# Windowed attention with four score buffers and a different order of work, and eleven small loads moved one stage earlier

## The reference

```
def neighbourhood_attention(u, rel_bias, na_idx, na_rel):
    ...
        sc = (jnp.einsum('bqhd,bqnhd->bhqn', qb, kb, preferred_element_type=jnp.float32) * scale
              + jnp.take(bias_flat, rel, axis=1))
        p = jax.nn.softmax(sc, axis=-1).astype(v.dtype)
        o = jnp.einsum('bhqn,bqnhd->bqhd', p, vb)
...
        oa = rms_norm(gqa_axial(...), g_out_a[l])
        ob = rms_norm(mla(...), g_out_b[l])
        oc = diff_attention(..., g_out_c[l], slopes, lambda_init)
        od = rms_norm(neighbourhood_attention(ud, d_rel_bias[l], na_idx, na_rel), g_out_d[l])
        mix = jnp.concatenate([oa, ob, oc, od], axis=-1) @ w_out[l]
        x = x + rms_norm(mix, norm_mix_post[l])
        h = rms_norm(x, norm_mlp_pre[l])
```

## Time and profile before

| what | value |
|---|---|
| median of 3 runs | 3023.75 us (3023.37 to 3025.94) |
| profiled execution | 3023.84 us, span 3022.0 us |
| PE, share of the span | 91% |
| DVE, ACT | 64%, 46% |
| stage D, layer 1 | 675.56 to 732.38 us |
| stage D, layer 2 | 2163.59 to 2220.43 us |
| idle time of PE before the output stage's first transposes | 12.3 us, 13.5 us |

### The profile page before, as it was taken

One profiled execution on the slowest core, in us unless ns is written; L12 is line 12 of the kernel. 1 busy time (PEld: TensorE's weight loads), 2 busy tenths in 40 slices (PEclk: granted clock), 3 DMA queues, 4 the chain that ended last, 5 costly groups with the idle time before them and its releaser, 6 DMA issues. The chain is left out here.

```text
span 3022.0 us, 37758 instructions
## 1 busy us (share of the span) xinstructions
PE 2740.4 (91%) x13872; PEld 2286.0 (76%) x13872; DVE 1931.9 (64%) x2856; ACT 1385.5 (46%) x2330; POOL 553.4 (18%) x487
## 2 busy tenths in 40 slices
PE   5998899887979999999879979988869799999997
PEld 4986888566758887888769859876658588878886
DVE  5612867886678887445774148669766888864457
ACT  4312766776343322443433147668654433334344
POOL 2122514780000000000021225248500000000000
PEclk7999999898989999999989989989989899999998
DMA  7232655543224444855533326754412244467555
GB/s 210 60 136 84 207 147 177 83 99 112 63 63 153 154 154 157 274 195 194 182 83 100 120 86 202 191 153 64 136 50 77 87 150 152 152 215 234 195 186 169
DMA packets 326941, 431.08 MB, mean 143 GB/s; under 512 B 82006, under 2 KB 207706, under 8 KB 326492
## 3 DMA queue, kind: packets, MB, share of 16 engines
q1 hardware_dynamic: 326736, 428.56, 46.1%
q10 hardware_dynamic: 12, 0.02, 0.0%
HBM read 288.00 MB, written 140.86 MB: 142 GB/s over the span
## 5 line engine op out<-in xcount | busy, mean ns | idle before, releaser
L1997 PE MATMUL f_ps<-dn_g 128*128 128x512 f32 x2688 | 617.1, 391 | 10.0 <-DVE dn_g L2228 10.0
L1997 PEld LDWEIGHTS f_ps<-dn_g 128*128 128x128 f32 x2688 | 505.4, 189 | 117.8 <-DVE dn_g L2228 7.2
L2228 DVE TENSOR_TENSOR dn_g<-dn_raw,dn_g 128x2048 fp32r<-128x2048 f32 x112 | 256.4, 2291 | 265.2 <-ACT dn_g L2077 265.2
L1987 PE MATMUL f_ps<-hc_h,up_w_h 128*128 128x512 f32 x896 | 352.5, 393 | 25.9 <-DVE up_w_l L2194 20.5
L2077 ACT ACTIVATE dn_g<-dn_raw 128x2048 fp32r<-128x2048 f32 x112 | 214.3, 1915 | 331.8 <-PE f_ps L1997 215.9
L1987 PE MATMUL f_ps<-hc_h,up_w_l 128*128 128x512 f32 x896 | 351.7, 393 | 0.0
L1987 PEld LDWEIGHTS f_ps<-hc_h,up_w_h 128*128 128x128 f32 x896 | 170.3, 190 | 63.1 <-DVE up_w_l L2194 27.5
L1987 PE MATMUL f_ps<-hc_ld,up_w_h 128*128 128x512 f32 x512 | 200.4, 391 | 0.0
L1987 PEld LDWEIGHTS f_ps<-hc_h,up_w_l 128*128 128x128 f32 x896 | 170.1, 190 | 35.8
L490 POOL TENSOR_TENSOR w_row_l<-w_row_first,w_row_h 128x512 fp32r<-128x512 f32 x12 | 14.9, 1281 | 904.4 <-ACT w_row_h L599 904.4
L1275 DVE CUSTOM_DVE_ANT_0 s_ps_c<-s_ps_c,distance 128x1024 f32<-128x1024 f32 x128 | 156.7, 1225 | 12.3 <-PE s_ps_c L1158 12.3
(11 more groups left out here) (297 smaller groups left out, 6461.7 us busy)
## 6 DMA issues: line engine op xcount, KB each, us to landing
act_blocks<-u_stage SPq DMA_DIRECT2D x32, 1792.0 KB, 6.6
dn_raw<-act_blocks SPq DMA_DIRECT2D x112, 512.0 KB, 3.9
mix<-in_w_down SPq DMA_DIRECT2D x128, 256.0 KB, 3.5
down_sums<-mix SPq DMA_DIRECT2D x128, 256.0 KB, 2.8
up_raw<-in_w_up SPq DMA_DIRECT2D x32, 1024.0 KB, 5.3
dn_raw<-down_sums SPq DMA_DIRECT2D x64, 512.0 KB, 4.8
dn_raw<-in_w_down SPq DMA_DIRECT2D x48, 512.0 KB, 4.6
w_raw<-in_w_in SPq DMA_DIRECT2D x16, 512.0 KB, 4.1
```

The source lines that it names most:

```text
L1987: last = nc.tensor.matmul(dst, wt[:, x % RING, k, :], tok, start=(opens[j] and k == 0 and i == 0), stop=(k == KT // 2 - 1 and i == 2), ski ...
L1997: last = nc.tensor.matmul(f_ps[:, bank0[pi] + i, :], lhs[:, n % 4, 0, q, i * P:(i + 1) * P], rhs[:, n % 4, 1, q, :], start=(down_opens[pi] ...
L2228: nc.vector.tensor_tensor(g_l[:, n % 4], dn_raw[:, n % 3], g_h[:, n % 4], ALU.subtract) \
```

## The change

D gets a stage function of its own, `window_stage`. The score tile is four buffers of one PSUM bank (before: two of two banks, of which 384 columns were used), `prob` has four buffers, and the waits follow from these. TensorE issues four `scores` first and then in each iteration turn(n), scores(n + 4), a half of `values`, `finish`; ScalarE runs two exponentials ahead and VectorE three maxima ahead. The eleven small loads are issued and waited for at the end of D's `fetch_out`; `g_col` and `out_li` have 1 KB of memory of their own for that. In the output stage VectorE multiplies `g_col` as its first instruction, with no wait.

```
+        def window_stage(mem, maps, tiles, mix_cols, mix, fetch, values_landed):
...
+            DEEP = 4
...
+                prob = mem.take("prob_d", [P, DEEP, 3 * P])
...
+                s_ps = ps(c, "s_ps_d", [P, DEEP, HALF])
+                t_ps = ps(c, "t_ps_d", [P, 2, HALF])
...
+                    def scores(n):
+                        m, i = n // NT, n % NT
+                        first, cnt = tiles[i][0:2]
+                        if n >= DEEP:
+                            pe.wait_ge(S["exp_done"], n - DEEP + 1)
...
+                    def turn(n):
+                        pe.wait_ge(S["exp_done"], n + 1)
+                        if n >= 2:
+                            pe.wait_ge(S["pt_lo"], n - 1)
...
+                    for n in range(DEEP):
+                        scores(n)
+                    for n in range(n_all + 4):
+                        if n < n_all:
+                            turn(n)
+                        if n + DEEP < n_all:
+                            scores(n + DEEP)
+                        if 0 <= n // 2 - 1 < n_groups:
+                            values(n // 2 - 1, n % 2)
+                        if n >= 4 and n % 2 == 0:
+                            finish(n // 2 - 2)
...
+                        act.wait_ge(S["max_done"], n + 1)
+                        if n >= DEEP:
+                            act.wait_ge(S["ptr_done"], n - DEEP + 1)
...
+                    exponential(0)
+                    exponential(1)
+                    for n in range(n_all + 2):
+                        if n + 2 < n_all:
+                            exponential(n + 2)
+                        if n < n_all:
+                            high(n)
+                        if n >= 3 and n % 2 == 1:
+                            lift(n // 2 - 1)
...
+                    for n in range(3):
+                        maximum(n)
+                    for n in range(n_all + 4):
+                        if n + 3 < n_all:
+                            maximum(n + 3)
+                        if n < n_all:
+                            low(n)
+                        if n >= NT + 3 and (n - 3) % NT == 0:
+                            divide((n - 3) // NT - 1)
...
+            oc = arena((136, 137))
+            g_col = oc.take("o_g_col", [P, KT])
+            out_li = oc.take("o_li", [P, 2])
...
                 for k in range(KT):
                     sp.dma_start(wo_raw[:, k, :], a["w_out"][layer][k * P:(k + 1) * P, :]).then_inc(S["w_landed0"], 16)
+                col = lambda v: v.rearrange("a p -> p a")
+                for j, name in ((0, "g_out_a"), (1, "g_out_b"), (3, "g_out_d")):
+                    for r in range(2):
+                        sp.dma_start(g_col[:, 2 * j + r:2 * j + r + 1], col(vec(name, r * P, (r + 1) * P))) \
+                            .then_inc(S["const_landed"], 16)
+                for j in range(2):
+                    for r in range(2):
+                        sp.dma_start(g_col[r * HD:(r + 1) * HD, 4 + j:5 + j], col(vec("g_out_c"))).then_inc(S["const_landed"], 16)
+                sp.dma_start(out_li[:, :], row_vector(vec("lambda_init"))).then_inc(S["const_landed"], 16)
                 sp.wait_ge(S["w_landed0"], 16 * KT)
+                sp.wait_ge(S["const_landed"], 16 * 11)
...
-            attention_stage("d", arena((-38, -24), (80, 104)), maps, tiles,
-                            lambda m: slice((12 + m) * HD, (13 + m) * HD), mix, fetch_out, 16)
+            window_stage(arena((-38, -24), (80, 104)), maps, tiles,
+                         lambda m: slice((12 + m) * HD, (13 + m) * HD), mix, fetch_out, 16)
...
-                om = arena((0, 48), (80, 92), (136, TOP))
+                om = arena((0, 48), (80, 92), (137, TOP))
...
-                g_col = om.take("o_g_col", [P, KT])
-                li = om.take("o_li", [P, 2])
...
-                    for j, name in ((0, "g_out_a"), (1, "g_out_b"), (3, "g_out_d")):
...
-                    sp.dma_start(li[:, :], row_vector(vec("lambda_init"))).then_inc(S["const_landed"], 16)
...
+                    nc.vector.tensor_scalar(g_col[:, 4:6], g_col[:, 4:6], out_li[:, 1:2], None, ALU.mult) \
+                        .then_inc(S["gain_done"], 1)
                     mix_sums(0)
-                    dve.wait_ge(S["const_landed"], 16 * 11)
-                    nc.vector.tensor_scalar(g_col[:, 4:6], g_col[:, 4:6], li[:, 1:2], None, ALU.mult) \
-                        .then_inc(S["gain_done"], 1)
                     mix_norm(0)
```

More of the change, by code:

```diff
@@ L1561, in _ @@
                 def _(sp):
-                    col = lambda v: v.rearrange("a p -> p a")
-                    for j, name in ((0, "g_out_a"), (1, "g_out_b"), (3, "g_out_d")):
[L1564 to L1569, removed]
-                    sp.dma_start(li[:, :], row_vector(vec("lambda_init"))).then_inc(S["const_landed"], 16)
                     def residual(t):
```

111 lines of the change are left out of this document (added).

## The result

The changed kernel takes 3003.11 us (median of 4 runs, 3001.53 to 3006.92), the kernel before beside it on the same chip 3023.56 us (4 runs, 3022.53 to 3025.94). The ratio is 0.9933, 95% interval 0.9916 to 0.9950: 20.45 us less, where 18.6 was forecast. The profiled execution took 3003.13 us with a span of 3001.5 us.

What follows compares the result with a forecast made beforehand. No engine is full: TensorE waits on a chain in D, and the output stage's reciprocal waits behind `o_li`. Savings of 12.0 (loads) and 6.6 (D), together 18.6, from 3023.8 give 3005 us, range 2998 to 3012.

Steps and rivals of the forecast that it cites:

- The likeliest case: Whole kernel: output stage and D both gain, 18.6 us together, giving 3005 us; chance 0.62.
- What bounds the kernel: In D, TensorE waits on a chain through ScalarE and VectorE; in the output stage, the first reciprocal stalls behind `o_li`.
- Loads moved, 12.0: Output stage: the first reciprocal waits only for the roots, saving 5.4 and 6.6 us in the two layers.
- D, 6.6: Stage D: the new order shortens waits before values, saving 3.3 us per layer, 1.06 per map.
- The chain of 1.44 us: In D, from an odd turn's end through ScalarE's copy and VectorE's subtraction to the values; claimed to stay the same.
- The buffers: Four one-bank score buffers and four `prob` in D: cost nothing; their possible effect on the clock was a rival.
- The chances: Whole kernel: forecast 0.62, rivals 0.16, 0.10, 0.08, 0.04; faster by over 0.2%: 0.95, cut to 0.93.
- the first three rivals: Only the output stage gains, 0.16; all of D's waits go, 0.10; the output stage gives part back, 0.08.
- Only the output stage gains: In D, ScalarE's exponentials delay the odd copies, so only the 12.0 us come: 3012 us; chance 0.16.
- All of D's waits go: In D, TensorE becomes the bound at 10.2 us per map, 14.2 saved there: 2997.6 us; chance 0.10.
- Part given back through the clock: Output stage: the 1.2 GHz stretch lasts longer as work comes earlier, 6 us back: 3011 us; chance 0.08.
- Slower, the clock falls in D: In D, many short gaps draw the clock down; with 60 us of low clock, 3035 us; chance 0.04.
- rival 4: The slower case: D's short gaps lower the clock, 3035 us with 60 us of it; chance 0.04.

Runs made afterwards that it cites:

- e1: The changed kernel with D's old stage function, so only the small loads and the g_col multiplication moved: 3011.33 us, ratio 0.9956.
- e2: The kernel before with only the new stage D, the small loads still in the output stage: 3016.80 us, ratio 0.9978.
- e5: The changed kernel with three score and prob buffers instead of four, maxima still three ahead: 3007.84 us, ratio 0.9954.
- e10: The changed kernel with two buffers, exponentials one ahead, and the maximum two tiles ahead in front of low on VectorE: 3008.23 us, ratio 0.9955.
- e3: The changed kernel with its four buffers and lookahead, but TensorE's old order, scores before turn: 3009.46 us, ratio 0.9955.
- e11: The changed kernel with three buffers and the maxima two instead of three tiles ahead, exponentials still two ahead: 3048.61 us, ratio 1.0089.
- e4: The changed kernel with two buffers, exponentials one ahead, and VectorE's maximum(n + 2) behind low(n): 3037.85 us, ratio 1.0050.
- e12: The changed kernel with V loaded in two halves and nothing else: 2995.52 us, ratio 0.9912.
- e8: The changed kernel with the fold ahead of the values, divide one tile earlier, and V loaded in two halves: 2994.75 us, ratio 0.9905.

## Why the prediction was right

The forecast was 3005 with a range of 2998 to 3012; 3003.1 was measured. The likeliest case is the one that came, and its two parts are shown apart by e1 and e2. Step by step:

- *What bounds the kernel.* The reading of two places by themselves held: both stalls went as described, and the rest of the kernel kept its times (D starts 0.2 us earlier in the first layer).
- *Loads moved, 12.0.* Measured 5.45 + 6.63 = 12.1 from D's end to the reciprocal; the first k matmul's load starts at 739.10 and 2217.13. The small loads cost D nothing (e1: 56.9 us). They did slow SP, one of their issues took 3.12 us, but SP's work ended at 691.7, long before D. The reciprocal was forecast 0.06 behind the roots; it is 0.03.
- *D, 6.6.* Measured 7.0 (3.6 and 3.4). The chain of 1.44 us did stay, the odd copies do start 0.31 after the turn's issue (0.30 forecast), the tail's three waits are 0.65, 0.66 and 0.68 and the fold's is 0.36, all as said. Within the map two terms were wrong, in opposite directions. The remaining waits were forecast as 0, 0, 0.20, 0.30 and 0.36, 0.86 together; they are 0.16, 0.27, 0.27, 0.38 and 0.36, 1.44, so that 4.7 us of waits before values are left in the first layer and not about 3. Of the 0.58, 0.4 is a wait that the prediction put at nothing without a reason, the one of the values for the lift: in the first two places what TensorE issues (1.40 and 1.29) covers the chain of `pt_l` (1.44 and 1.20) but for 0.04, as forecast, and the lift ends last, since the new order puts nothing more between a half of values and the next. The prediction had the lift coming later, but asked only what that does to ScalarE. The other 0.2 is thinner filling. For TensorE's own issue was taken as unchanged at 12.10 - 1.92 = 10.18; it is 11.10 - 1.44 = 9.66. By the starts of the loads the eight turns of a map take 2.23 instead of 2.87, the folds 1.59 instead of 1.79, the values 3.54 instead of 3.26 and the scores 2.30 instead of 2.26. The turns stand behind values of 128 columns or fold matmuls now: the earlier trace rows have 0.39 us from the start of a turn of three to the next load, the rows after 0.34 and 0.28. So 0.58 more waiting and 0.52 less issue left the map only 0.06 off. The main mechanism, one scores more against a chain of the same length, was right; that the sum came so close is luck.
- *The buffers.* I wrote that their cost is nothing by the rows, and that is so, but I gave them no benefit either. e5 and e10 show that with three or two buffers a map takes 11.72: the order gives the gain only if the maximum that stands ahead of `low` doesn't wait for scores just issued. Depth alone gives nothing (e3).
- *The edges and behind.* From D's start to the MLP's first weight load the layers are 10.0 and 10.3 us shorter. D and the stall make 3.6 + 5.45 = 9.0 and 3.4 + 6.63 = 10.0, which leaves 1.0 and 0.3. The stretch at 1.2 GHz in the output stage is 1.45 us shorter in the first layer (8.15 against 9.60) and 0.34 in the second (8.22 against 8.56), which at half the clock is worth at most 0.7 and 0.2. A second low stretch follows around the second tile's transposes: some 10 us of it in the first layer before (mean clock 0.68 from 760 to 776), some 6.7 in its second layer and in both after (0.79 over 16 us). That the 1.0 and 0.3 come from these stretches is argued, not tried.
- *The chances.* The forecast and the first three rivals add to 0.96, not to the 0.95 from which 0.93 was taken; nothing hangs on it.

The rivals. *Only the output stage gains* (3012): refuted by e2, and ScalarE's exponentials don't delay the odd copies. *All of D's waits go* (2997.6): refuted, 4.7 us are left before the values in the first layer. *Part given back through the clock*: the low stretch in the output stage became shorter, the opposite. *Slower, the clock falls in D*: the map after runs at 1.00 with its five gaps of 0.16 to 0.38 us. The Trainium skill's page "TensorE: Matmul & The Clock Gate" (section "A second HAM failure mode: psum-queue depth-cycling") tells of one bf16 kernel with 512 columns a matmul, whose clock oscillated as it cycled through PSUM banks; here, with fp32 and four banks taken in turn, it did not. What rival 4 feared does exist: in e11 the clock fell in the inner maps, but they were as long with little of it as with much. The slower kernels here, e4 and e11, are slower in D through a ring of waits between VectorE and ScalarE. The prediction named no such case: its only slower rival was the clock.

What stays open: why the turn's issue is shorter behind narrower matmuls (seen in the rows, not tried by itself), what the wait for the lift costs (read from the rows, not tried by itself), and why the clock rose early in some layers.

## What to carry to other kernels

When an engine waits for a chain through other engines, measure the chain from the end of the issue that starts it to the start of the one that needs it, and count what the waiting engine issues in between; moving independent work into that gap is worth its issue time, up to the wait (e3 against the change: 1.0 us per map for one exchange of two lines). Do the same for every other semaphore that the load waits for: here the lift was hidden behind the wait that went. In these kernels the order served best when each engine's lookahead was longer than that of the engine it feeds: with VectorE's only as long as ScalarE's, e5's gain of 0.5% became e11's loss of 0.9%, and with TensorE's only as long as VectorE's, 0.6 of the 1.0 us per map went (e5). Small loads that a stage's first instruction waits for belong in the stage before (12.4 us, e1), and a large load whose first part is enough to begin belongs in two halves (e12).

## What the runs showed of the hardware that I had not expected

- A wait can cost more than its length. In the changed kernel TensorE stood 2.56 us until V landed; 1.35 us later (683.75 to 685.10) the granted clock fell to 0.50, 1.2 GHz, for 3.2 us of dense work. The profiles of all twelve kernels with V whole show it in both layers, after waits of 2.4 to 4.0 us: 24 times of 24 the clock fell 0.6 to 1.6 us behind V's first load, for 3.2 to 3.4 us, however long the wait was. In the two kernels with V in halves (e8, e12), where the waits were 1.1 to 1.8 us in two pieces, it stayed at 1.00 in all four layers.
- The clock's fall need not cost anything: e11's maps took 17.53 or 17.54 us at a mean clock of 0.81 and of 0.90.
- The same matmuls in another order take another time to issue: 10.18 us per map before and 9.66 after, with the same 83 instructions; the turns alone account for 0.64 less.
- Eleven small loads, queued behind 6 MB of large ones, landed 5.0 to 13.1 us after their issue and held SP's queue for up to 3.12 us in one issue. Under a stage of 53 us that was free.
